# HGRN2 scan: the eight masked Gram matrices of a chunk are summed on VectorE and multiplied with the values once

## The reference

```python
def step(state, blk):
    qc, kc, vc, lc = blk
    cum = jnp.cumsum(lc, axis=2)
    rel = cum[:, :, :, None, :] - cum[:, :, None, :, :]
    dec = jnp.exp(jnp.where(lower, rel, -jnp.inf))
    att = jnp.einsum('bhtc,bhtsc,bhsc->bhts', qc, dec, kc)
    out = (jnp.einsum('bhts,bhsv->bhtv', att, vc)
           + jnp.einsum('bhtc,bhcv->bhtv', qc * jnp.exp(cum), state))
    last = cum[:, :, -1:, :]
    state = (jnp.exp(last[:, :, 0, :, None]) * state
             + jnp.einsum('bhsc,bhsv->bhcv', kc * jnp.exp(last - cum), vc))
    return state, out
```

## Time and profile before

| | |
|---|---|
| median of 3 runs | 5172.91 us (5163.15 to 5174.36) |
| the profiled execution's own time | 5142.85 us |
| its span, first to last instruction | 5141.0 us |
| mean granted TensorE clock | 0.897 of full |
| scan stage (first transposes at L1121 to last L1108) | 559.6 to 814.0 us |
| busy in the span: PE, DVE, ACT, POOL | 4198.6, 3266.5, 1323.8, 1419.4 us |
| masking, L1085, in all | 48 instructions, 58.5 us |
| values times masked matrices, L1157, in all | 768 in the trace (384 matmuls), 98.2 us |

### The profile page before, as it was taken

The page is one execution under the profiler, slowest core; times in us unless marked ns, Lnnn a source line. Parts: engine busy times, 40 slices in busy tenths (PEclk is TensorE's granted clock), DMA queues, the critical chain, the costliest instruction groups (busy, mean ns, idle before and its releaser), DMA issues. The chain is left out here.

```text
span 5141.0 us, 59219 instructions
## 1 busy us (share of the span) xinstructions
PE 4198.6 (82%) x21780; PEld 3188.4 (62%) x21780; DVE 3266.5 (64%) x6621; ACT 1323.8 (26%) x2531; POOL 1419.4 (28%) x1387
## 2 busy tenths in 40 slices
PE   6977688779999998587888777756789998777786
PEld 5864687676666666344544463534678887666675
DVE  3145774319997778577887823493349967555565
ACT  2125222213444655000000021421223565400000
POOL 0000331003332445344444300060004334344341
PEclk8989898889999999698999887957889999988997
DMA  4120101237987999999999710133249999899995
GB/s 165 58 76 31 40 5 33 90 116 290 320 330 266 402 404 414 361 391 384 390 392 389 294 32 19 18 103 82 66 153 375 336 347 414 335 405 402 403 403 232
DMA packets 469170, 1254.78 MB, mean 244 GB/s; under 512 B 52094, under 2 KB 191092, under 8 KB 463252
## 3 DMA queue, kind: packets, MB, share of 16 engines
q0 software_dynamic: 184320, 671.17, 33.9%
q1 hardware_dynamic: 277944, 570.82, 30.4%
q10 hardware_dynamic: 6620, 9.01, 0.5%
HBM read 1147.59 MB, written 103.25 MB: 243 GB/s over the span
## 5 line engine op out<-in xcount | busy, mean ns | idle before, releaser
L1942 PE MATMUL banks<-acts_in,v_rows 128*128 128x384 f32 (+1 forms) x4096 | 1164.1, 447 | 300.7 <-DMA v_rows<-peer_v 173.2
L1942 PEld LDWEIGHTS banks<-acts_in,v_rows 128*128 128x128 f32 x4096 | 799.4, 197 | 665.1 <-DMA v_rows<-peer_v 193.9
L1565 PE MATMUL banks<-h_dense,u_t 128*128 128x384 f32 (+1 forms) x4096 | 1200.0, 437 | 0.0
L1539 POOL DMA_INDIRECT rows<-peer_u,expert x640 | 633.1, 989 | 1619.2 <-DVE weight L1842 805.8
L1565 PEld LDWEIGHTS banks<-h_dense,u_t 128*128 128x128 f32 x4096 | 748.3, 193 | 246.0 <-issue 2.4
L1842 DVE CUSTOM_DVE_ANT_0 rows<-rows,banks 128x1024 f32<-128x1024 f32 x640 | 765.4, 1211 | 194.1 <-DMA rows<-peer_u,expert 129.6
L1924 POOL DMA_INDIRECT v_fetched<-peer_v,expert x640 | 606.8, 948 | 861.1 <-DVE banks L2004 746.7
L2004 DVE SCALAR_TENSOR_TENSOR banks<-v_fetched,weight,banks 128x1024 f32<-128x1024 f32 x630 | 784.1, 1281 | 0.0
L1980 DVE TENSOR_TENSOR acts_in<-acts_in,gates 128x384 f32<-128x384 f32 (+1 forms) x256 | 124.8, 488 | 430.8 <-DMA acts_in<-activations 430.6
L1933 ACT COPY y_tok<-banks 128x1024 f32<-128x1024 f32 x5 | 5.1, 1012 | 1461.4 <-DVE banks L2004 1461.4
L1624 ACT COPY u_t<-banks 128x512 f32<-128x512 f32 x512 | 299.9, 586 | 289.2 <-PE banks L1556 286.4
(11 more groups left out here) (444 smaller groups left out, 5688.6 us busy)
## 6 DMA issues: line engine op xcount, KB each, us to landing
u_raw<-peer_u SPq DMA_DIRECT2D x256, 512.0 KB, 7.9
v_rows<-peer_v SPq DMA_DIRECT2D x256, 512.0 KB, 15.2
gate_table<-part SPq DMA_DIRECT2D x20, 2048.0 KB, 11.7
activations<-acts SPq DMA_DIRECT2D x128, 192.0 KB, 5.8
gates<-gate_table SPq DMA_DIRECT2D x8, 3072.0 KB, 22.8
acts_in<-activations SPq DMA_DIRECT2D x128, 192.0 KB, 12.2
peer_wq_in<-peer_wq SPq DMA_DIRECT2D x16, 1024.0 KB, 5.3
ada_ring<-ada_w SPq DMA_DIRECT2D x32, 512.0 KB, 4.1
```

Source lines behind the costliest of these rows:

```text
L1539: pool.indirect_dma_start(out=ring[:, s % U_RING, :], out_offset=None, in_=rows_of_u, in_offset=bass.IndirectOffsetOnAxis(ap=expert[:, t, ...
L1565: last = nc.tensor.matmul(out, u_t[:, i % 2, k * P:(k + 1) * P], h[:, k], start=(k == 0), stop=(k == DK - 1))
L1942: return nc.tensor.matmul(y_at(m if RESIDENT else j // GROUP * DK + m), v[:, j % V_ROWS, m * P:(m + 1) * P], acts[:, j % V_ROWS], start=st ...
```

## The change

VectorE writes the masked matrices to a new buffer `masked`, waits for that, and adds the eight matrices by one `tensor_reduce` over a view that puts the matrix number innermost: it reads 1,024 numbers per partition, eight for each output column, 128 columns (512 bytes) apart. The 128 columns that come out are `pairs`, and TensorE multiplies them with the values once instead of eight times. There is one buffer `masked`, so a mask also waits for the reduction before it.

```diff
-        pairs = a.sb("pairs", [P, 2, NL * P])
+        masked = a.sb("masked", [P, NL * P])
+        pairs = a.sb("pairs", [P, 2, P])
...
                     if n >= 2:
                         dve.wait_ge(out_ready, n - 1)
-                    nc.vector.tensor_tensor(pairs[:, n % 2], ps[:, GRAM + (n % 2) * 1024:GRAM + (n % 2) * 1024 + 1024],
-                                            masks[:], ALU.mult).then_inc(pairs_ready, 1)
+                    if n:
+                        dve.wait_ge(pairs_ready, n)
+                    own(nc.vector.tensor_tensor(masked[:], ps[:, GRAM + (n % 2) * 1024:GRAM + (n % 2) * 1024 + 1024],
+                                                masks[:], ALU.mult))
+                    own.settle()
+                    nc.vector.tensor_reduce(out=pairs[:, n % 2], in_=masked[:].rearrange("p (e t) -> p t e", t=P),
+                                            op=ALU.add, axis=AX.X).then_inc(pairs_ready, 1)
...
-                    for e in range(NL):
-                        last = nc.tensor.matmul(ps[:, OUT:OUT + P], v, pairs[:, n % 2, e * P:(e + 1) * P],
-                                                start=(i == 0 and e == 0), stop=(e == NL - 1))
-                    last.then_inc(out_ready, 1)
+                    nc.tensor.matmul(ps[:, OUT:OUT + P], v, pairs[:, n % 2], start=(i == 0), stop=True)\
+                        .then_inc(out_ready, 1)
```

## The result

The changed kernel takes 5240.63 us, the median of 5 runs (5237.08 to 5248.84), against 5172.91 us (5163.15 to 5177.75) before: a ratio of 1.0137 with a 95% interval of 1.0124 to 1.0150, 67.7 us slower. The forecast was 5246 us.

What follows compares the result with a forecast made beforehand. VectorE was taken as the path in units 0 to 6, then the chain between units. 95.0 - 2.1 - 3.4 - 9.0 - 12.2 = 68.3, plus 4.7 for the clock: 73 us slower, 5246 us; range 5207 to 5272.

Steps and rivals of the forecast that it cites:

- What bounds: In units 0 to 6 VectorE is the path from first mask to L1051, then the chain; TensorE-pace rival 0.03.
- the chain: Between units: L1051, exponential, L1024, transposes, Gram matrices, begun when VectorE's preparation ends; 7.24 us of idle VectorE.
- The reduction: VectorE's added sum of 1,024 strided numbers takes 1.95 us; dearer rival 2.3 us, chance 0.11.
- The choice between 1.21 and 1.95 us: Reduction time with the stride free (rival, 5214 us, chance 0.15) or paid for (forecast, chance 0.67).
- What a chunk costs more: VectorE's mask, settle and reduction take 3.11 instead of 1.13 us: 1.98 us more, 48 chunks, 95.0 us.
- GpSimd's hold: GpSimd's multiplications hold up VectorE's preparation; with the reduction ahead, that is partly freed: 3.4 us back.
- Direction 1: L1108's waits for the last and first chunk's eight matmuls, 2.90 and 0.59 us, disappear: 9.0 us back.
- The last unit: Paced by TensorE at 22.7 us before, by VectorE at 22.4 us after: 12.2 us back.
- The clock: TensorE, less busy in the scan, may run at its lower level; 4.7 of a possible 7.8 us taken as cost.
- the 0.5 to 0.7 that I had named as a sign: Sign of being right: TensorE's granted clock in the scan near 0.5 to 0.7.
- The 0.6 us a unit start: Lower clock lengthens transposes to first mask from 4.51 to 5.09 us at unit starts: 7 x 0.6 = 4.1 us.
- the 5.1 us that I had named as a sign of being wrong: Sign of being wrong: unit starts longer than 5.1 us from transposes to mask.

Runs made afterwards that it cites:

- e2: The kernel before with one of the eight values matmuls and no sum; ratio 0.9978, scan 234.2 us against 249.3.
- e3: The changed kernel with the one values matmul made eight times on the summed matrix; ratio 1.0148 to the kernel before, scan 323.9 us.
- e9: The kernel before with the next unit's preparation steps 2, 2, 2, 2, 1, 0 behind the chunks instead of 1, 2, 1, 2, 1, 2; ratio 0.9975.
- e1: The changed kernel with the reduction reading eight adjacent numbers (wrong sum); ratio 1.0088 to the kernel before, reduction 1.22 instead of 1.90 us.
- e4: The changed kernel with measured reductions and masks at various steps in SBUF and PSUM added behind the scan; ran once, 5279.41 us.
- e8: The kernel before with the next unit's preparation steps 3, 2, 2, 2, 0, 0 behind the chunks instead of 1, 2, 1, 2, 1, 2; ratio 0.9997.
- e10: The changed kernel with its stride moved to PSUM and preparation steps 3, 2, 2, 2, 0, 0; ratio 1.0067 to the kernel before.
- e7: The kernel before with each level computed, masked (576 columns) and multiplied for 64 queries instead of 128; ratio 1.0146, scan 319.3 us.
- e5: The changed kernel with the mask reading PSUM strided and the reduction reading adjacent numbers, same sum; ratio 1.0102 to the kernel before.

## Why the prediction was right

The forecast was 73 us; the scan took 67.3 us more, the medians 67.7. Point by point:

- **What bounds.** VectorE from first mask to last step, then the chain. Shown by e2 (TensorE's matmuls gone: 15 us) and e3 (put back: 7 us), and by e9 for the chain, where a part of the gain is the clock.
- **The reduction.** 1.95 us forecast, 1.90 measured: 48 x 0.05 = 2.4 us of the 5.7 us that the forecast was too high. The choice between 1.21 and 1.95 us, which decided most of the size, rested on one reduction of 128 numbers and one copy; e1 and e4 show that it was the stride.
- **What a chunk costs more.** 1.98 us forecast; 1.88 us in the chunk shown. The settle costs 0.03 us as in the earlier trace rows (603.59 + 1.23 against 604.85).
- **GpSimd's hold.** L1052 takes 0.95 us in units 0 to 3, where it took 2.00 (in units 4 to 6 it took 0.95 already). L1047 gave back 2.0 us in all, and 3.6 moved onto L1066 (27.8 us in all before, 31.4 after). That is 4.2 + 2.0 - 3.6 = 2.6 us back, 3.4 forecast. Units 0 to 3 grew by 10.3 us each (41.4 instead of 31.0); the forecast without the clock was 11.9 - 0.3 - 0.7 = 10.9.
- **Direction 1.** The wait of 2.90 us is gone, and units 4 to 6 grew by 8.6 us each (42.8 instead of 34.2), less than the others, as the sum had it (8.4).
- **The last unit.** 22.8 us where it was 22.7 and 22.4 was forecast: VectorE paces it now, 3.5 us a chunk.
- **The clock** is the term that was mis-sized: 4.7 us, of which 2.1 came. The level did fall, 0.93 to 0.76 over the scan, though not to the 0.5 to 0.7 that I had named as a sign. The 0.6 us a unit start came from a base of 4.51 us between transposes and first mask, which is the highest of the seven values before; their mean is 4.34. After the change they are 4.20 to 5.15, mean 4.65, and two of them pass the 5.1 us that I had named as a sign of being wrong by 0.05. So the starts cost 2.1 us instead of 4.1 (VectorE's idle time there went from 49.5 to 51.6). The last unit, down for 3.7 us, lost nothing: its Gram matrices from the third chunk on ran at the upper level, 14 passes in 1.73 us. I had taken somewhat over half of the two, and that one of them came to nothing was not foreseen.
- **A wait that I had not named:** TensorE's L1160 waits 17.9 us in all for ScalarE's copy of the output, which stands behind an exponential in ScalarE's queue. VectorE's waits for TensorE outside the unit starts are so short (1.2 us) that it can have cost hardly anything.

Also, TensorE does not wait for the state in every chunk, as I had written, but in 35 of 48. The total agrees, but most of its terms are a little high: 2.6 us too much for the clock, some 2.4 for the reduction, and less than 1 for the rest.

My expectations failed in the experiments where I had left out a cost: for the steps 3, 2, 2, 2, 0, 0 (e8, and with them e10) the waits that they open inside a unit, and for passes of 64 columns (e7) the clock and the fact that such a pass is no shorter.

## What to carry to other kernels

Two engines without a gap in the same timeline are not both the bound: ask which one the other waits for over a whole round of the outer loop, and cut each one's work alone (one run each) before trading one for the other. A trade of 1.56 us a chunk of the engine that has slack for 1.9 us of the one that has none lost 67 of the second's 91 us here. Where VectorE must read across matrices, put the large step on the PSUM side and keep the numbers in SBUF adjacent or two apart.

## What the runs showed of the hardware

- VectorE, float32, 1,024 numbers: 1.22 us at steps of 4 and 8 bytes in SBUF, 1.97 us at 16 and 32, 1.86 us at 64 to 512 (e4). Writes with a step cost the same within 0.03 us (1.23 us at 8 bytes, 1.97 at 16, 1.89 at 512). PSUM reads cost 1.22 us at steps of 4, 8, 16 and 512 bytes, and the same at 512 bytes while TensorE writes PSUM (e5, mean of 48).
- TensorE, float32, weight loads of 128 columns (e7): 14 passes with 64 moving columns took 1.67 to 1.73 us at the upper level and 3.09 to 3.19 at the lower, 14 with 128 columns 1.73 and 3.19.
- In e7, after 3.91 us without a matmul, the passes of 64 columns stayed at the lower level for about 24 us with hardly a gap, and the granted clock of the first 40 us was 0.64 (TensorE busy 36.92 us); with passes of 128 columns it was 0.90 in the same stretch (busy 35.61 us). Which of the two, the short matmuls of the Gram matrices or those of the values, goes with it was not tried apart.
- After 1.52 us without a matmul the next ones ran at the upper level, after 3.74 us at the lower, and 14 passes took 1.73 or 3.19 us (e3).
